# Reordering the start of the two h stages of a hybrid mLSTM / attention / ConvFFN layer: an own bank for tile 0, halves of unit 0, gates and late transposes spread over the first units

## The reference

```python
h = rmsnorm(x, g_pre_mix)                 # (256, 2048)
proj = h @ w_in                           # heads, gates m_if (16 columns), merge gates
i_pre, f_pre = split(proj[m_if] + b_gates)
F = cumsum(log_sigmoid(f_pre)); m = running max          # stabiliser of the mLSTM
...                                       # mLSTM and differential attention, 8 heads each
x = x + rmsnorm(mix @ w_out, g_post_mix)
h = rmsnorm(x, g_pre_ffn)
u = causal_dwconv(h @ w_up)
x = x + rmsnorm((gelu(gate) * val) @ w_down, g_post_ffn)
```

## Time and profile before

| what | value |
|---|---|
| runs | 1859.86, 1860.45, 1860.62 us (median 1860.45) |
| the profiled execution | 1860.45 us |
| its span, first to last instruction | 1858.6 us |
| TensorE busy | 1837.3 us, 99% of the span |
| VectorE, ScalarE, GpSimd busy | 59%, 48%, 4% |

### The profile page before, as it was taken

One profiled execution on the slowest core, in us unless ns is written; L12 is line 12 of the kernel. 1 busy time (PEld: TensorE's weight loads), 2 busy tenths in 40 slices (PEclk: granted clock), 3 DMA queues, 4 the chain that ended last, 5 costly groups with the idle time before them and its releaser, 6 DMA issues.

```text
span 1858.6 us, 35703 instructions
## 1 busy us (share of the span) xinstructions
PE 1837.3 (99%) x13796; PEld 1743.8 (94%) x13796; DVE 1098.9 (59%) x1313; ACT 895.5 (48%) x1161; POOL 68.4 (4%) x90
## 2 busy tenths in 40 slices
PE   7999999999999999999999999999999999999998
PEld 7999999999999999999999889999999999988886
DVE  5666456555655565545454557676666667755555
ACT  6554444444544444444434446555555555544443
POOL 2800000000000000000000000000000000000000
PEclk9999999999999999999999999999999999999999
DMA  7565655565555555555555664666666666565554
GB/s 237 181 200 172 188 183 176 173 193 178 177 172 189 181 178 173 189 195 194 187 194 195 243 209 137 194 197 191 198 192 191 193 192 191 192 216 194 193 194 141
DMA packets 164496, 351.44 MB, mean 189 GB/s; under 512 B 11048, under 2 KB 11328, under 8 KB 163776
## 3 DMA queue, kind: packets, MB, share of 16 engines
q1 hardware_dynamic: 162768, 344.11, 57.5%
q10 hardware_dynamic: 1280, 5.08, 0.7%
q0 software_dynamic: 368, 1.09, 0.2%
HBM read 348.12 MB, written 2.12 MB: 188 GB/s over the span
## 4 chain that ended last, share of the span: by engine, by line
PE 97%; DVE 1%; DMA 1%; issue 1%; ACT 1%; POOL 0%; DVEq 0%; SPq 0%; POOLq 0%; ACTq 0%
PE ps L1191 26%; PE ps L1189 26%; PE ps L1190 26%; PE ps L1371 11%; PE ps L1375 5%; PE ps L1256 1%; PE ps L1331 1%; DMA gm<-in_x 0%; PE ps L1264 0%; PE ps L1308 0%; PE ps L1224 0%; DVE x L846 0%; DMA raw<-in_w_out 0%; ACT act L571 0%; PE ps L1307 0%
## 5 line engine op out<-in xcount | busy, mean ns | idle before, releaser
L850 DVE TENSOR_TENSOR w_lo<-raw,w_hi 128x1024 fp32r<-128x1024 f32 x638 | 778.2, 1225 | 661.8 <-ACT w_hi L540 659.5
L540 ACT ACTIVATE w_hi<-raw 128x1024 fp32r<-128x1024 f32 x640 | 677.6, 1062 | 775.7 <-PE ps L1191 612.0
L1189 PE MATMUL ps<-h,w_hi 128*128 128x256 f32 x3200 | 886.5, 277 | 0.0
L1191 PE MATMUL ps<-h,w_lo 128*128 128x256 f32 x3200 | 883.8, 276 | 0.0
L1190 PE MATMUL ps<-h,w_hi 128*128 128x256 f32 x3200 | 883.8, 276 | 0.0
L1190 PEld LDWEIGHTS ps<-h,w_hi 128*128 128x128 f32 x3200 | 600.8, 188 | 0.5
L1189 PEld LDWEIGHTS ps<-h,w_hi 128*128 128x128 f32 x3200 | 600.7, 188 | 0.5
L1191 PEld LDWEIGHTS ps<-h,w_lo 128*128 128x128 f32 x3200 | 600.7, 188 | 0.0
L1371 PE MATMUL ps<-w_hi,ks_hi 128*128 128x512 f32 x448 | 174.6, 390 | 0.3 <-DVE ks_lo L846 0.2
L1375 PE MATMUL ps<-w_lo,ks_hi 128*128 128x512 f32 x448 | 174.4, 389 | 0.0
L1371 PE MATMUL ps<-w_hi,ks_lo 128*128 128x512 f32 x448 | 138.1, 389 | 0.0
(11 more groups left out here) (165 smaller groups left out, 1377.1 us busy)
## 6 DMA issues: line engine op xcount, KB each, us to landing
raw<-in_w_in SPq DMA_DIRECT2D x288, 512.0 KB, 3.5
raw<-in_w_up SPq DMA_DIRECT2D x176, 512.0 KB, 4.3
raw<-in_w_down SPq DMA_DIRECT2D x88, 512.0 KB, 4.6
raw<-in_w_branch_m SPq DMA_DIRECT2D x32, 512.0 KB, 4.6
raw<-in_w_branch_a SPq DMA_DIRECT2D x32, 512.0 KB, 4.4
raw<-in_w_out SPq DMA_DIRECT2D x32, 512.0 KB, 4.6
x<-in_x ACTq DMA_DIRECT2D x1, 2048.0 KB, 11.7
gm<-in_x SPq DMA_DIRECT2D x2, 512.0 KB, 4.8
```

The costliest lines, as they stand in the source:

```text
L540: return nc.scalar.activation(out_ap, in_ap, ACT.Copy, scale=scale)
L850: nc.vector.tensor_tensor(w_lo[:, at:at + UNIT], raw[:, slot, :], w_hi[:, at:at + UNIT].bitcast(F32), ALU.subtract).then_inc(lo_done, 1)
L1189: nc.tensor.matmul(out_ap, stat_hi, mov_hi, start=start, stop=False, skip_group_check=True)
L1191: return nc.tensor.matmul(out_ap, stat_lo, mov_hi, start=False, stop=stop, skip_group_check=True)
```

## The change

Tile 0 of h goes to bank 7 alone, so that `h_psum` and `h_hi_done` count it by itself (groups 0, 1, 2-3, 4-5, ...). At the start TensorE transposes the identity 18 times ahead of the first rows, and repeats 8 transposes between b=0 and b=1; of the b=1 tiles it does 0 to 7, then gates 0 and 1, then unit 0 in two halves, of which the first waits for `first_lo`. The other transposes are put ahead of the gates of units 1 and 2, and two gates stand ahead of each of units 0 to 7. ScalarE and VectorE split unit 0 behind two tiles, in halves of 512, and units 1, 2 and 3 behind tiles 4, 6 and 12. `gate_rows` moves from u=1 to 8, `gate_exponents` from 4 to 11, `gate_sums` from 2 to 9, `lambda_dots` from 3 to 9, `lambda_full` from 6 to 13. 128 columns instead of 65 of the channel table are loaded first. In the middle, b=0 tiles run in the order 1 to 9, 0; unit 0 starts behind tile 0 alone; the other transposes stand behind unit 0 and unit 1; the partial sums of the second norm and the splits are put in another order on VectorE.

```diff
-            return (2, 3, 4, 5, 6, 2, 3, 4)[k // 2]
+            return 7 if k == 0 else (2, 3, 4, 5, 6, 2, 3, 4)[k // 2]
...
+            def split_first():
+                scalar.wait_ge(raw_loaded[0], 16)
+                scalar.wait_ge(pe_done, 1)
+                copy(w_hi[:, away(0):away(0) + 512], raw[:, 0, 0:512]).then_inc(first_hi, 1)
+                copy(w_hi[:, away(0) + 512:away(0) + UNIT], raw[:, 0, 512:UNIT]).then_inc(hi_done, 1)
...
-            norm_tiles(0, C_GPM, lambda: split(0, 0, 0, away(0)), 6)
-            split(0, 1, 1, away(1))
-            split(0, 2, 2, away(2))
+            norm_tiles(0, C_GPM, {2: split_first, 4: lambda: split(0, 1, 1, away(1)), 6: lambda: split(0, 2, 2, away(2)),
+                                  12: lambda: split(0, 3, 3, away(3))})
...
-            normed(1, gm_rows, gm_rows, 0, range(3))
+            normed(1, gm_rows, gm_rows, 0, range(2))
...
+            def split_first():
+                normed(1, gm_rows, gm_rows, 0, range(2, 4))
+                for c, hi, lo, n in ((0, first_hi, first_lo, 1), (512, hi_done, lo_done, 1)):
+                    at = away(0) + c
+                    vec.wait_ge(hi, n)
+                    nc.vector.tensor_tensor(w_lo[:, at:at + 512], raw[:, 0, c:c + 512], w_hi[:, at:at + 512].bitcast(F32),
+                                            ALU.subtract).then_inc(lo, 1)
...
-            normed(0, xn, x1, TB, range(2, 4))
-            mean_square(ROW_PIECES_OF[1], X_MS, x_ms, len(ROW_PIECES), x_sum)
-            normed(1, xn, x1, TB, range(3))
-            norm_tiles(KT, C_GPF, {2: lambda: normed(1, xn, x1, TB, range(3, 4)), 4: lambda: split(BASE_UP + 1, 1, away(1)),
-                                   6: lambda: split(BASE_UP + 2, 2, away(2)), 10: lambda: split(BASE_UP + 3, 3, away(3))})
+            residual_sums = ROW_PIECES_OF[1], X_MS, x_ms, len(ROW_PIECES)
+            normed(0, xn, x1, TB, range(2, 3))
+            partial_sum(*residual_sums, 1)
+            normed(0, xn, x1, TB, range(3, 4))
+            partial_sum(*residual_sums, 2)
+            full_sum(*residual_sums, x_sum)
+            normed(1, xn, x1, TB, range(2))
+            def second_split():
+                split(BASE_UP + 1, 1, away(1))
+                normed(1, xn, x1, TB, range(3, 4))
+            norm_tiles(KT, C_GPF, {2: lambda: normed(1, xn, x1, TB, range(2, 3)), 4: second_split,
+                                   6: lambda: split(BASE_UP + 2, 2, away(2)), 8: lambda: split(BASE_UP + 3, 3, away(3))})
...
+            def tiles_before(src, count, u):
+                if u == 1:
+                    for k in range(FIRST, EARLY):
+                        tile(src, count, k, 1)
+                    late_tiles(src, count, 10)
+                if u == 2:
+                    late_tiles(src, count, 12)
+                    late_tiles(src, count, 14)
...
+            for i in range(18):
+                nc.tensor.transpose(ps[:, 0, 0:P], ident, ident)
+            for k in range(EARLY):
+                tile(gm_rows, 0, k, 0)
+            again(gm_rows, 8)
+            for k in range(FIRST):
+                tile(gm_rows, 0, k, 1)
...
+                    if g == 0 and u < UNITS_CHUNK:
+                        tiles_before(gm_rows, 0, u)
+                        for k in (2 * u, 2 * u + 1):
+                            last = gate_tile(k)
+                        if u == UNITS_CHUNK - 1:
+                            last.then_inc(gates_psum, 1)
+                    if g == 0 and u == 0:
+                        pe.wait_ge(first_lo, 1)
+                        unit_channels(0, 0, h_hi, h_lo, range(0, 1))
+                        ready(0)
+                        unit_channels(0, 0, h_hi, h_lo, range(1, 2))
+                        continue
...
+                    ready(g * U_UP + (BASE_UP + u))
                     if first and u < UNITS_CHUNK:
-                        pe.wait_ge(h_done, KT + 2 * u + 2)
...
+                        tiles_before(xn, KT, u)
+                        for kk in range(2):
+                            pe.wait_ge(h_done, KT + 2 * u + kk + 1)
+                            unit_channels(u, 0, h_hi, h_lo, range(kk, kk + 1))
+                        continue
```

More of the change, by code:

```diff
@@ L625, in mix_turn @@
                 for u in range(U_MIX):
-                    split_ahead(g, U_MIX, BASE_MIX, u, home_mix)
-                    if first and u == 1:
+                    if u or not first:
+                        split_ahead(g, U_MIX, BASE_MIX, u, home_mix)
+                    if first and u == 8:
                         gate_rows()
-                    if first and u == 4:
+                    if first and u == 11:
                         gate_exponents()
@@ L868, in _, with partial_sum, full_sum @@
                 nc.vector.sem_inc(starts_at_one, 1)
-            def mean_square(pieces, column, ready, before, done):
+            def partial_sum(pieces, column, ready, before, j):
                 first = stat[:, column + pieces[0]:column + pieces[0] + 1]
[L873 to L876, removed]
+                vec.wait_ge(ready, before + pieces[j] + 1)
+                nc.vector.tensor_scalar(first, first, stat[:, column + pieces[j]:column + pieces[j] + 1], None, ALU.add)
+                vec.drain()
+            def full_sum(pieces, column, ready, before, done):
+                first = stat[:, column + pieces[0]:column + pieces[0] + 1]
                 i = pieces[-1]
@@ L879, in mean_square @@
                 nc.vector.tensor_scalar(first, first, stat[:, column + i:column + i + 1], EPS, ALU.add, ALU.add).then_inc(done, 1)
+            def mean_square(pieces, column, ready, before, done):
+                for j in range(1, len(pieces) - 1):
+                    partial_sum(pieces, column, ready, before, j)
+                full_sum(pieces, column, ready, before, done)
             def normed(b, dst, src, count, quarters=range(4)):
@@ L1194, in ready, with unit_channels @@
                 pe.wait_ge(lo_done, n + 1 + RING)
-            def unit_channels(u, pair, a_hi_t, a_lo_t):
-                for kk in range(2):
+            def unit_channels(u, pair, a_hi_t, a_lo_t, rows=range(2)):
+                for kk in rows:
                     k = 2 * (u % UNITS_CHUNK) + kk
@@ L1225, in tile, with again @@
                                           src[:, b, k * P:(k + 1) * P], ident)
-                if b and k % 2:
+                if b and ends_group(k):
                     ins.then_inc(h_psum, 1)
[L1229 to L1241, removed]
+            def again(src, times):
+                for i in range(times):
+                    k = 1 + i % (FIRST - 1)
+                    nc.tensor.transpose(ps[:, tile_bank(k), k % 2 * T:k % 2 * T + P], src[:, 0, k * P:(k + 1) * P], ident)
             def late_tiles(src, count, k):
@@ L1270, in _, with gate_tile @@
             pe.wait_ge(ident_loaded, 16)
[L1271 to L1278 removed]
+            for i in range(18):
[5 more added lines that the diff above has]
+                tile(gm_rows, 0, k, 1)
+            pe.wait_ge(wif_ready, 1)
+            def gate_tile(k):
                 pe.wait_ge(h_done, k + 1)
                 nc.tensor.matmul(ps[:, 7, 0:T], hm_hi[:, k, 0:P], h_hi[:, k, :], start=k == 0, stop=False, skip_group_check=True)
[L1281 removed]
+                return nc.tensor.matmul(ps[:, 7, 0:T], hm_hi[:, k, 0:P], h_lo[:, k, :], start=False, stop=k == KT - 1,
                                         skip_group_check=True)
[L1283 removed]
             for g in range(TURNS_MIX):
@@ L1418, in _ @@
             rows_phase(TURNS_OUT, U_OUT, BASE_OUT, 0, out_banks)
-            early_tiles(xn, KT)
+            for k in (*range(1, EARLY), 0):
+                if k in (4, 8, 0):
+                    pe.wait_ge(gained, {4: 3, 8: 4, 0: 5}[k])
+                if k == FIRST:
+                    again(xn, 44)
+                tile(xn, KT, k, 0)
+            for k in range(FIRST):
+                tile(xn, KT, k, 1)
             def up_turn(g, first):
```

67 lines of the change are left out of this document (33 added, 34 removed).

## The result

The changed kernel takes **1862.64 us** (median of 20 runs, 1861.09 to 1864.80), the kernel before beside it 1860.14 (20 runs, 1858.97 to 1861.15, and one of 1897.68). The ratio is 1.0014, with a 95% interval of 1.0008 to 1.0020: slower, by less than the 0.2% named above. 1859.7 was forecast with 1858.4 to 1861.6 around it. The profiled execution took 1864.4 us, 1862.6 of it the span, 4.0 more than the span before; the forecast was 0.7 less.

A forecast was written before the change was run, and what follows sets the result against it. TensorE, busy 1837.3 of 1858.6 us, was taken as the bound, so only its idle or slow stretches could gain. 1860.45 - 0.07 (start) - 0.66 (middle) = 1859.7 us, range 1858.4 to 1861.6.

The forecast's parts named there:

- The start's hand-overs: Start: ScalarE begins at 13.33 us, VectorE at 13.83, TensorE's unit 0 at 16.26; the start gains 0.07 us.
- "I take nothing" for the pace behind interleaved gates: Units 1 to 7 at the start: slower or faster matmul spacing behind two gates each was counted as zero.
- the bound of +1.3: Start: the most lost if units 1 to 7 all ran at the slow spacing, +0.19 us each.
- The middle: Middle: unit 0 starts behind tile 0 alone, winning 0.88 us; 0.22 goes back to later transposes, net -0.66 us.
- The rival that the gain does not arrive: Middle: unit 1's weight or slow spacing behind gates eats the gain; around 1860.3 us, up to 1861.0; 17%.
- The gate chain ... a wait of TensorE: Unit 33: longer GpSimd steps make `a_rs` late and hold its split; 1861.7 us at 4.8 us extra; 10%.
- the end of the chain: GpSimd's gate chain, begun 19 us later, was to end at 109.5 us, with `a_rs` at 111.6.
- The cover of 2.8 us: Unit 33: its split is ready at 114.4 us and TensorE wants it at 117.2, leaving 2.8 us.
- The deciding point: Unit 33: from 2.8 us of extra chain length on, each further microsecond is TensorE's.
- In its new place it meets VectorE's softmax work: The later gate chain on GpSimd meets a few softmax steps, making it 1 to 2 us longer, without reaching TensorE.
- Full pace is there at 12.97 now: Start: early transposes bring TensorE to full pace by 12.97 us, where before it came close to 17 us.
- the rival that identity transposes do not raise the clock: Start: TensorE stays slow until 16.98 us (1860.2 us) or for 4 us from unit 0's start (1861.9); 8%.

The follow-up runs named there:

- e3: The changed kernel with all gates ahead of units 0 to 3 and the gate steps at units 3, 4, 5 and 7; 1860.11 us.
- e4: The changed kernel with its start put back in the order of before (tile 0's bank and longer table load stay); 1859.19 us, then 1859.36.
- e7: The changed kernel with 27 more identity transposes in TensorE's three idle stretches ahead of unit 0; 1861.68 us.
- e1: The kernel before with only the gate steps moved late, to units 8, 9, 11 and 13; 1862.23 us.
- e2: The changed kernel with GpSimd's loop written out and its drains, the root's among them, replaced by a semaphore; 1862.44 us.
- e5: The changed kernel without the 18 identity transposes and the 8 repeats; 1863.10 us.
- e10: e4 with the 18 identity transposes ahead of its first transposes; 1859.24 us.
- changed again: The changed kernel run once more with nothing altered; 1862.28 us.

## Why the prediction was wrong

- **The start's hand-overs: right.** Forecast was unit 0 at 16.26 us, with VectorE's chain as the limit and TensorE idle; measured 16.36, and TensorE idle 0.89 just ahead of it.
- **"I take nothing" for the pace behind interleaved gates: mis-sized.** +0.40 to unit 8 in the changed kernel, +0.30 in its second profile. It is the spacing for the most part: in five of units 1 to 7 the matmuls stand 0.118 apart, not 0.113, and in two of them before. It lies inside the bound of +1.3 and should have been taken with a third of it. Early gates (e3) have it too, at +0.18.
- **The middle: the mechanism right, the sum a little off.** Won 0.86 (0.88); the net is -0.48 in the changed kernel and -0.27 to -0.48 in the others, instead of -0.66; the missing 0.2 to 0.4 is the same spacing for the most part, in unit 2 and, in six of the profiles, in the two behind it. The rival that the gain does not arrive is refuted by the traces, e4's two among them; the times alone can't tell.
- **"The gate chain ... a wait of TensorE": the rival was the truth, and its working had two holes.** I had the end of the chain right (109.5, measured 108.8) and reasoned from there that `a_rs` comes at 111.6. The root's own duration was taken from the earlier trace rows, where its drain had nothing to wait for. Behind the chain's loads the root takes 8.3 us instead of 2.1, so `a_rs` comes at 117.1, 5.5 later than forecast. The cover of 2.8 us and the 1.9 by which TensorE was late itself leave the 0.8 measured at unit 33 (0.3 to 3.2 in the other profiles of this chain with its drain). The deciding point that I gave for this rival was right; the extra length that I expected, 1 to 2 us, was the wrong kind: I looked for it in GpSimd's steps, which took 43.6 or 46.6 us in all against 46.3 before, and it sat in a synchronising instruction.
- **"In its new place it meets VectorE's softmax work" was read one way only.** I priced what VectorE does to GpSimd and not what GpSimd does to VectorE. The two splits went from 2.45 to 3.43 us and the `prob` pair from 0.75 to 1.60, ahead of a reader that TensorE waits for: +1.43 at unit 24 (+0.39 in the second profile of the changed kernel and +0.41 in e7, 1.42 to 1.44 in e1, e2 and e5), the larger of the two waits in the changed kernel, and one that no sentence of the prediction names. The rule that I cited (the Trainium skill, GPSIMD Engine Reference, section 1: shared interfaces, contention with VectorE instructions that have two inputs in SBUF) speaks of contention between the two. The trace agrees, in both directions: a split went from 1.23 to 1.72 us, and GpSimd's step at L511 from 0.84 to 1.70 beside it.
- **"Full pace is there at 12.97 now": right, but it need not stay.** In all eight profiles with identity transposes the clock was up by 8.2 to 10.8 us. In one of them, e2, it fell again at 15.0, which cost 2.3 us, and two runs of e3 point the same way. Of the rival that identity transposes do not raise the clock nothing is left: e10 against e4 differs by them alone, and the transposes behind them take 0.11 instead of 0.21. The sentence of the Trainium skill (TensorE: Matmul & The Clock Gate, Part 4) that the full clock doesn't engage for transposes is not what these traces show.
- **The sum.** By the first profile 1860.1 + 0.4 + 1.4 + 0.8 - 0.5 is 1862.2, measured 1862.64. By the second, 1860.3 + 0.3 + 0.4 + 1.1 - 0.5 is 1861.6; its own run took 1861.73, the median is 1862.28. The rest is scatter of the two waits, of the projections' weights and, in some runs, perhaps the clock. The range ended at 1861.6 since it priced one wait of TensorE where there are two.

## What to carry to other kernels

A chain that is moved later costs what it meets, in both directions: lay its instructions beside the other engine's work at the new place, and price each side. Behind a batch of loads that GpSimd issues, a drain on GpSimd is not the cheap one of an idle queue; pass values by semaphore there, or keep the last steps off the path. And where TensorE is raised to full clock early, holes behind it are a risk: one profile here shows the clock lost again. Transposes of the identity into a free bank filled them in three kernels without such a case, but they must not run into the work that follows.

## What the runs showed of the hardware

- **A drain of GpSimd behind loads issued from its own queue** took 7.01, 6.38, 4.69, 5.37 and 6.92 us (changed, e1, changed again, e7, e5), and 0.83 where the last load had been issued 14 us before (e3). In all five it ended 0.5 us after the last load of `um` had landed (landed at 115.6, 115.5, 114.6, 117.3 and 117.7; next instruction at 116.0, 116.0, 115.1, 117.7 and 118.2). With a semaphore in its place GpSimd went on after 0.08 us, 5.9 us before that load landed (e2). So the drain waits for the loads.
- **GpSimd slows VectorE.** A split of 128x1024 with two inputs took 1.23 us alone and 1.72 (half of 3.43) beside GpSimd's steps of 8x256; the smaller two-input step 0.38 and 0.80. How the two meet differs between executions of one kernel: two splits took 3.43 us in one profile of the changed kernel and 2.88 in the next.
- **TensorE's clock can fall back soon after it rose.** In e2 it rose at 8.2 us, during the 18 transposes of the identity, fell at 15.0, after TensorE had been idle for 1.4 us up to 12.9 and for 0.5 up to 14.5, and came back at 21.8, with TensorE busy from 16.2. The same instructions of TensorE kept it in both profiles of the changed kernel (up from 9.5 and 8.6).
- **The spacing of 128x256 matmuls** is 0.113, 0.118 or 0.120 us with TensorE never waiting. The same unit has 0.113 in one profile and 0.118 in another (unit 1 of the changed kernel again, and of e7). What sets it was not found. The slow one holds in 16 to 21 of the 640 units of a profile; among units 0 to 8 it holds in 7 in the changed kernel and in 3 before.
